# A hybrid four-mixer trunk on one core: segment decays by ScalarE's rectifier, state-space chunks two slots later, a weight panel split earlier, decay sums moved, and the first input transposed by quarters

## The reference, cut to what matters

```python
cs = jnp.cumsum(dt * a, axis=2)
seg = cs_t[..., :, None] - cs_t[..., None, :]
decay = jnp.exp(jnp.where(causal, seg, -jnp.inf))
y_intra = jnp.einsum('bcgjls,bcsgjp->bclgjp', cb[:, :, :, None] * decay, xdt)
```

## Time and profile before

| | us |
|---|---|
| median of 3 runs (lowest to highest) | 1979.54 (1978.78 to 1980.86) |
| the profiled execution | 1979.62 |
| its span, first to last instruction | 1977.6 |
| TensorE (PE) busy | 1930.4 (98% of the span) |
| VectorE (DVE) busy | 1164.7 (59%) |
| ScalarE (ACT) busy | 965.1 (49%) |
| GpSimd (POOL) busy | 491.9 (25%) |
| mean granted TensorE clock | 0.995 of full |

### The profile page before, as it was taken

The page is one execution under the profiler, slowest core; times in us unless marked ns, Lnnn a source line. Parts: engine busy times, 40 slices in busy tenths (PEclk is TensorE's granted clock), DMA queues, the critical chain, the costliest instruction groups (busy, mean ns, idle before and its releaser), DMA issues.

```text
span 1977.6 us, 27606 instructions
## 1 busy us (share of the span) xinstructions
PE 1930.4 (98%) x11112; PEld 1055.3 (53%) x11112; DVE 1164.7 (59%) x1475; ACT 965.1 (49%) x1796; POOL 491.9 (25%) x298
## 2 busy tenths in 40 slices
PE   7999999999999999999999999999999999999998
PEld 3446665455456665544454466654554556655443
DVE  5677676477435765534366777663873366764432
ACT  5674433356325666533356743433653356665331
POOL 0213445043212231121002143541331222221110
PEclk9999999999999999999999999999999999999999
DMA  6224232333334443243211242323433343432431
GB/s 190 81 96 127 98 117 76 117 98 106 107 101 123 123 118 91 87 148 131 68 65 65 96 139 90 113 94 103 118 102 106 101 135 91 123 107 86 140 106 43
DMA packets 204520, 208.92 MB, mean 106 GB/s; under 512 B 28688, under 2 KB 193514, under 8 KB 204394
## 3 DMA queue, kind: packets, MB, share of 16 engines
q1 hardware_dynamic: 204394, 207.17, 33.3%
HBM read 181.91 MB, written 2.16 MB: 93 GB/s over the span
## 4 chain that ended last, share of the span: by engine, by line
PE 84%; DVE 8%; ACT 4%; issue 3%; DMA 1%; SPq 0%; POOL 0%; DVEq 0%; ACTq 0%
PE PS L553 82%; DVE wsp L1259 2%; DVE M L1259 2%; DVE X L1262 1%; PE PS L741 1%; PE PS L659 1%; ACT X L965 1%; DVE ys L1259 1%; PE PS L791 1%; DVE Y L1262 0%; DVE ys L1437 0%; ACT wsp L962 0%; ACT M L995 0%; DMA xres<-x 0%; ACT Y L965 0%
## 5 line engine op out<-in xcount | busy, mean ns | idle before, releaser
L553 PE MATMUL PS<-hT,wsp 128*128 128x512 f16 (+2 forms) x4968 | 1086.1, 377 | 5.1 <-DVE wsp L1259 5.1
L553 PEld LDWEIGHTS PS<-hT,wsp 128*128 128x128 f16 x4968 | 479.9, 98 | 563.1 <-issue 14.0
L1259 DVE SCALAR_TENSOR_TENSOR wsp<-stage,wsp 128x2048 f16<-128x2048 f32 x148 | 377.0, 2547 | 197.8 <-ACT wsp L962 195.1
L553 PE MATMUL PS<-ys,wsp 128*128 128x512 f16 x1536 | 340.4, 379 | 0.0
L962 ACT ACTIVATE wsp<-stage 128x2048 f16<-128x2048 f32 x148 | 281.6, 1903 | 84.2 <-PE PS L553 81.9
L553 PEld LDWEIGHTS PS<-ys,wsp 128*128 128x128 f16 x1536 | 149.6, 98 | 176.4 <-issue 3.0
L553 PE MATMUL PS<-wsp,hT 128*128 128x256 f16 x1728 | 195.5, 273 | 0.0
L553 PEld LDWEIGHTS PS<-wsp,hT 128*128 128x128 f16 x1728 | 168.9, 98 | 22.9 <-issue 2.3
L1601 POOL TENSOR_TENSOR X<-X,K 128x1024 f32<-128x1024 f32 x26 | 63.4, 2440 | 366.7 <-DMA X<-X 366.7
L1601 POOL TENSOR_TENSOR M<-M,T 128x512 f32<-128x512 f32 x48 | 67.4, 1409 | 348.7 <-DVE T L1259 348.7
L965 ACT ACTIVATE X<-PS 128x512 f32<-128x512 f32 x120 | 68.9, 595 | 133.6 <-PE PS L553 99.9
(11 more groups left out here) (197 smaller groups left out, 2107.8 us busy)
## 6 DMA issues: line engine op xcount, KB each, us to landing
stage<-w_in SPq DMA_DIRECT2D x120, 1024.0 KB, 4.9
stage<-w_branch SPq DMA_DIRECT2D x32, 1024.0 KB, 5.1
X<-X SPq DMA_DIRECT2D x120, 128.0 KB, 2.3
stage<-w_out SPq DMA_DIRECT2D x8, 1024.0 KB, 5.3
Y<-sums SPq DMA_DIRECT2D x8, 512.0 KB, 5.8
M<-sums SPq DMA_DIRECT2D x8, 512.0 KB, 5.8
Y<-Y SPq DMA_DIRECT2D x24, 128.0 KB, 2.4
xres<-x SPq DMA_DIRECT2D x4, 512.0 KB, 6.7
```

The costliest lines, as they stand in the source:

```text
L553: return pe.matmul(o, a, b, start=start, stop=stop, skip_group_check=True)
L1259: return dve.scalar_tensor_tensor(out=o, in0=a, scalar=c, in1=b, op0=op0, op1=op1)
```

## The change

- The rows of sums go to ScalarE: eight rectifiers a chunk (`falls`) make max(0, cs of the partition - cs of the column), in place, with a scale of -1 and cs as per-partition bias; the exponential then has the scale -1. Where the mask is one this is the same value; elsewhere it is exp(0) = 1, which the masked C.B product multiplies by zero. POOL's `segments` is gone. `falls` of the next chunk stands at the end of ScalarE's slot.
- Chunks move to slots 18 to 21 and 23 to 26, the ends of the groups to 22 and 27.
- The decay sums move from slot 3 to slot 9, with SyncE's write and reads of the rows, and the waits on their readers from the gates of slot 4 to the transposes of slot 10.
- Panel 2 is split in slot 0, after both evacuations; the softplus chain comes after it on VectorE, and on ScalarE too.
- The input: the first quarter of x is loaded ahead of the constants, ScalarE copies the column parameters after the first square, TensorE transposes six blocks quarter by quarter.
- In `DIFF_END` slots the dummy exponential comes right after the square root, and `rotated_hi` after the squares.

The list of semaphores and the counts per layer, which follow from this, are left out.

```diff
@@ -91,8 +91,8 @@
 ROTATED = ("kc", "qc", "qd", "kd")
-SSD_SLOT = [16, 17, 18, 19, 21, 22, 23, 24]
-SSD_END = {20: 0, 25: 1}
+SSD_SLOT = [18, 19, 20, 21, 23, 24, 25, 26]
+SSD_END = {22: 0, 27: 1}
 TURN_OF = {SLOT[("conv", _i)] + (2 if _i == 8 else 1): _i for _i in (8, 0, 2, 4, 6)}
@@ -106,9 +106,9 @@
 
-SUMS_IN = SLOT[("ga", 1)]
+SUMS_IN = SLOT[("conv", 10)]
 ROWS_OUT_AT = SUMS_IN + 5
-ROWS_IN_AT = {SLOT[("vc", 0)] + 1: 0, SLOT[("vc", 0)] + 3: 1}
+ROWS_IN_AT = {SUMS_IN + 6: 0, SUMS_IN + 7: 1}
 ROWS_IN_AT.update({SSD_SLOT[_q] + 3: _q + 2 for _q in range(6)})
@@ -153,7 +153,9 @@
 
-    if p == 0 or p + 1 >= OUT0:
+    if p == 0:
+        return range(LOAD_OF[2], LOAD_OF[3])
+    if p == 1 or p + 1 >= OUT0:
         return range(0)
@@ -460,10 +462,11 @@
         def _(sp):
-            sp.dma_start(K[:, 0:K_COS], consts[:, 0:K_COS]).then_inc(s["consts_in"], 16)
-            load_columns(sp, 0)
             for q in range(ST):
                 sp.dma_start(xres[:, q, :], x[0, q * P:q * P + P, :]).then_inc(x_in[q], 16)
+                if q == 0:
+                    sp.dma_start(K[:, 0:K_COS], consts[:, 0:K_COS]).then_inc(s["consts_in"], 16)
+                    load_columns(sp, 0)
             sp.dma_start(stage[:, 0], panel_source(0, 0)).then_inc(s["first_in"], 16)
@@ -713,8 +716,8 @@
                     if p == SUMS_IN:
-                        pe.wait_ge(s["lru_v"], at("lru_v", 2, layer))
-                        pe.wait_ge(s["lru_w"], at("lru_w", 2, layer))
+                        pe.wait_ge(s["lru_v"], at("lru_v", 8, layer))
+                        pe.wait_ge(s["lru_w"], at("lru_w", 8, layer))
                         pe.wait_ge(s["dta_ready"], at("dta_ready", 1, layer))
@@ -764,9 +767,6 @@
                                 pe.wait_ge(s["dta_ready"], at("dta_ready", 1, layer))
-                            if t == 2:
-                                pe.wait_ge(s["dec_ready"], at("dec_ready", 1, layer))
-                                pe.wait_ge(s["cs_rows"], at("cs_rows", 1, layer))
                             if t >= 2:
@@ -781,7 +781,8 @@
                             if n == 0:
-                                pe.wait_ge(s["lru_w"], at("lru_w", 8, layer))
+                                pe.wait_ge(s["dec_ready"], at("dec_ready", 1, layer))
+                                pe.wait_ge(s["cs_rows"], at("cs_rows", 1, layer))
                             if n >= 2:
@@ -840,21 +841,27 @@
 
-                    if k == 0:
-                        pe.wait_ge(s["xn_ready"], at("xn_ready", 4, 0))
-                        pe.wait_ge(s["first_cols"], at("first_cols", 2, 0))
-                    if k >= 6:
-                        pe.wait_ge(s["whole_lo"], k - 5)
+                    pe.wait_ge(s["whole_lo"], k - 5)
                     for q in range(ST):
...
 
+                def turn_quarter(q):
+
+                    pe.wait_ge(s["xn_ready"], at("xn_ready", q + 1, 0))
+                    if q == 0:
+                        pe.wait_ge(s["first_cols"], at("first_cols", 2, 0))
+                    for k in range(6):
+                        one = pe.transpose(whole_at(k)[:, P * q:P * q + P], Mseq[:, q, k * P:k * P + P], ident)
+                        if q == ST - 1:
+                            one.then_inc(s["whole_T"], 1)
+
                 def first_product():
...
                         return wsp[:, 0, h, k, P * u:P * u + P]
-                    for k in range(6):
-                        turn_whole(k)
+                    for q in range(ST):
+                        turn_quarter(q)
                     pe.wait_ge(s["first_hi"], at("first_hi", 1, 0))
@@ -932,8 +939,8 @@
             square_x(0)
+            start_columns(act, 0)
             square_x(1)
-            start_columns(act, 0)
             square_x(2)
@@ -1017,10 +1024,10 @@
                         q = SSD_SLOT.index(p)
-                        act.wait_ge(s["ssd_tri"], at("ssd_tri", q + 1, layer))
                         if q > 0:
                             act.wait_ge(s["ssd_out"], at("ssd_out", q, layer))
-                        act.activation(est, seg[q % 2], ACT.Exp).then_inc(s["ssd_exp"], 1)
+                        act.wait_ge(s["ssd_fall"], at("ssd_fall", q + 1, layer))
+                        act.activation(est, seg[q % 2], ACT.Exp, scale=-1.0).then_inc(s["ssd_exp"], 1)
                     if p in SSD_END:
@@ -1085,6 +1092,7 @@
                         act.activation(mean, mean, ACT.Sqrt, scale=1.0 / P, bias=eps).then_inc(s["df_sq"], 1)
+                        act.activation(small[:, 100:101], eps, ACT.Exp)
 
@@ -1142,10 +1150,10 @@
                             copy(Y_HI[1][:, f, :], PS[:, 4 + t, :], colB[:, B_NG + f:B_NG + f + 1]).then_inc(s["yb_hi"], 1)
-                    if p > 0 and PANELS[p - 1][0] in ROTATED:
+                    turned = p > 0 and PANELS[p - 1][0] in ROTATED
+                    if turned and p not in DIFF_END:
                         rotated_hi(p)
                     if p in DIFF_END:
-                        act.activation(small[:, 100:101], eps, ACT.Exp)
                         act.wait_ge(s["df_nT"], at("df_nT", 2 * DIFF_END[p] + 2, layer))
@@ -1156,6 +1164,8 @@
                                 .then_inc(s["df_or"], 1)
+                    if turned and p in DIFF_END:
+                        rotated_hi(p)
 
@@ -1170,7 +1180,22 @@
 
+                def falls(q):
+
+                    g, c = divmod(q, 4)
+                    act.wait_ge(seg_in[q % 2], at("seg_in0", 16 * (q // 2 + 1), layer))
+                    if q == 0:
+                        act.wait_ge(s["cs_ready"], at("cs_ready", 1, layer))
+                    for j in range(8):
+                        last = act.activation(seg[q % 2][:, j, :], seg[q % 2][:, j, :], ACT.Relu, scale=-1.0,
+                                              bias=cs[:, c, 8 * g + j:8 * g + j + 1])
+                    last.then_inc(s["ssd_fall"], 1)
+
                 def after(p):
+                    if p + 1 == SSD_SLOT[0]:
+                        falls(0)
+                    if p in SSD_SLOT[:-1]:
+                        falls(SSD_SLOT.index(p) + 1)
                     if SWA0 < p <= SWA0 + 8:
@@ -1191,15 +1216,21 @@
                     local_turned(p)
-                    for n in splits_in(p):
-                        split_hi(n)
+                    if p > 0:
+                        for n in splits_in(p):
+                            split_hi(n)
                     before(p)
                     evacuate(p, 0)
+                    if p == 0:
+                        evacuate(p, 1)
+                        for n in splits_in(p):
+                            split_hi(n)
                     between(p)
...
                         turned_hi(act, nxt, 0)
-                    evacuate(p, 1)
+                    if p > 0:
+                        evacuate(p, 1)
                     after(p)
@@ -1549,9 +1580,14 @@
                     evacuate(p, 0)
+                    if p == 0:
+                        evacuate(p, 1)
+                        for n in splits_in(p):
+                            split_lo(n)
                     between(p)
                     middle(p)
-                    evacuate(p, 1)
+                    if p > 0:
+                        evacuate(p, 1)
                     after(p)
@@ -1607,17 +1643,6 @@
 
-                def segments(q):
-
-                    g, c = divmod(q, 4)
-                    here = cs[:, c, 8 * g:8 * g + 8].unsqueeze(2).to_broadcast([P, 8, P])
-                    if q == 0:
-                        pool.wait_ge(s["cs_ready"], at("cs_ready", 1, layer))
-                    pool.wait_ge(seg_in[q % 2], at("seg_in0", 16 * (q // 2 + 1), layer))
-                    tt(seg[q % 2], seg[q % 2], here, ALU.subtract).then_inc(s["ssd_diff"], 1)
-                    pool.wait_ge(s["ssd_diff"], at("ssd_diff", q + 1, layer))
-                    tt(seg[q % 2], seg[q % 2], tri.unsqueeze(1).to_broadcast([P, 8, P]), ALU.mult).then_inc(s["ssd_tri"], 1)
-
                 def rotated_lo(p):
@@ -1662,10 +1687,6 @@
                         tt(xw, xdt, head(dend[:, c, hs]), ALU.mult).then_inc(s["ssd_x"], 1)
-                        if q < 7:
-                            segments(q + 1)
-                    if p + 1 == SSD_SLOT[0]:
-                        segments(0)
                     if p > 0 and PANELS[p - 1][0] in ROTATED:
```

More of the change, by code:

```diff
@@ L125 @@
     "rope_stack": 576, "rows_in": 16, "second_in": 16, "sp_exp": 1, "sp_in": 1, "ssd_T": 8, "ssd_exp": 8, "ssd_g": 8,
-    "ssd_mt": 8, "ssd_norm": 2, "ssd_out": 8, "ssd_read": 8, "ssd_ss": 2, "ssd_st": 6, "ssd_tri": 8, "ssd_diff": 8, "ssd_x": 8,
+    "ssd_mt": 8, "ssd_norm": 2, "ssd_out": 8, "ssd_read": 8, "ssd_ss": 2, "ssd_st": 6, "ssd_fall": 8, "ssd_x": 8,
     "ssd_y": 8, "step_in": 16, "sw_T": 16, "sw_Ta": 16, "sw_e": 16, "sw_m": 16, "sw_n": 16, "sw_o": 16, "sw_s": 16,
@@ L341, in program @@
```

(6 more changed lines are left out.)

## The result

The changed kernel takes 1946.2 us (median of 4 runs, 1944.91 to 1947.35) against 1979.16 us for the kernel before, run beside it (4 runs): ratio 0.9833, 95% interval 0.9816 to 0.985. The forecast was 1950. The profiled execution took 1947.35 us, its span is 1945.4 us, and the span is 32.2 us shorter than before.

A forecast was written before the change was run, and what follows sets the result against it. TensorE was taken as the bound, with 47.2 us idle and low-clock matmuls to win. Terms 0.9 + 0.6 + 3.0 + 7.6 + 10.6 + 7.0 = 29.7 us off 1979.6 gave 1950, range 1945 to 1963.

The forecast's parts named there:

- What bounds it: TensorE, busy 1930.4 of 1977.6 us; the change can win only from 47.2 us idle time and low-clock matmuls.
- Start: Input loads and transposes by quarters: three quarters transposed while x arrives, first products end earlier; gain 0.9 us.
- Panel 2: Split in slot 0: gain 0.6 us in layer 0, 3.0 in layer 1 after a new 2.0 us step-size wait.
- Decay sums: Moved to slot 9: removes the 2.00 us waits and slow gates of slot 4 in both layers; gain 7.6 us.
- Chunks: State-space stages: later slots and segments off POOL remove TensorE's waits there in both layers; gain 10.6 us.
- I count all 10.6 us: State-space waits, all counted as gone: 5.0 + 2.0 before transposes, 2.2 before normalized outputs, 1.4 for low halves.
- Rectifiers: Eight a chunk on ScalarE: 2.5 us, within 4.3 us of room before TensorE takes up the chunk's result.
- The slower rival: ScalarE bounds the chunks: TensorE waits at ten late chunks' exponentials above 0.54 us a rectifier, 1987 at 1.0 us; chance 0.03.
- Head pairs: Slots 53 and 57, both layers: earlier table load and later rotary copies remove four 1.74 us waits; gain 7.0 us.
- VectorE and the place had made the chunks late: Rival for the chunks: VectorE, not POOL's segments, made them late; gives back 5 to 10 us, 1955 to 1961; chance 0.20.
- a wait takes the place of each one removed: Rival, at slot 4's gates and head-pair ends: new waits replace the old, about 1963 to 1975; chance 0.10.

The follow-up runs named there:

- Run 7: Changed kernel with panel 2 split in slot 1 again instead of slot 0: 1949.02 us.
- run 2: Changed kernel with the chunks back in slots 16 to 19 and 21 to 24, rectifiers kept on ScalarE: 1954.22 us.
- run 3: Changed kernel with the segments back on POOL in the new slots, no rectifiers on ScalarE: 1952.45 us.
- run 8: Changed kernel with each rectifier in two halves of 64 columns, sixteen a chunk: 1953.64 us.
- the better version: Changed kernel with chunk 4's rectifiers at the end of slot 22 and slot 2's gates asked for four k-steps later: 1940.16 us (median of 5 runs).
- run 6: Changed kernel with the decay sums back in slot 3, row loads left in their new slots: 1952.6 us.
- run 12: Changed kernel unchanged, executed again beside the better version: 1946.63 us (4 runs).

## Why the prediction was right, and where it wasn't

**What bounds it**: right. The gain is idle time of TensorE (24.3 us) and shorter busy time (7.9 us), most of it low clock.

**Start**: I took 0.9 us of gain, with -1.0 to +1.0 as bounds. It is 1.1 with the products at full clock and 0 with them at the low one; the loss of 1.0 did not come. The step that three quarters of the transposes are done while x still arrives was wrong: one quarter is (six at 7.00 us), since the second quarter's square could start at 9.50 us only and the last three come together.

**Panel 2**: the chain of steps held, with the split ahead, the softplus late and a new wait of 2.0 us (2.2 measured). The size was off by the clock: I forecast net 3.0 with 5.0 as the bound for a clock that stays up; it stayed up in the first execution, 4.7, and fell in the second, 4.7 - 1.8 = 2.9. Run 7 gives 3.1 for the split's place alone; the rest of the 4.7 is the early evacuation of tile 1, which I had not priced by itself, and how long the low clock lasted.

**Decay sums**: 8.0 for 7.6, and nothing late behind their new place in slot 9. Undone, 7.7, of which 6.2 at the gates of slot 4.

**Chunks**: the step "I count all 10.6 us" failed in one term and was short in another. The term that failed is L799's 2.2 us: I let the wait for the normalized outputs go with POOL's segments, and did not ask what the rectifiers of the next chunk stand in front of at the end of group 0. It is there now with 1.73 us a layer, 3.9 us in time. I had read `evacuate` as passing at once where VectorE takes the tile; it does not. That this stage still gained 11.6, close to the 10.6, is luck: two things that I had not priced made up for it. A wait costs 0.2 to 0.4 us more than its length, and in the kernel before, the 1.98 us wait in layer 1 slot 17 had low clock behind it (the 15 us window there reads 0.89), which I had looked for at slot 4 only:

```profile
1221.03 1.06 PE L791 MATMUL PS<-K,M 128*128 128x128 f32 x8 [1.98 <-DVE Y L1262]
1221.93 2.67 PE L553 MATMUL PS<-hT,wsp 128*128 128x512 f16 x6
```

Six such products took 1.47 us at full clock, in slot 2 of layer 0. The reason given, POOL beside VectorE, is the smaller half of the stage's gain (runs 2 and 3); the larger is the place.

**Rectifiers**: 2.43 us a chunk for 2.5; no reload of a table; room of 4.1 us for 4.3, as run 8 shows. The slower rival (over 0.54 us each) had its place wrong as well: with sixteen instructions the queue becomes too long at the end of group 0, not at a chunk's exponential. By the rule of the Trainium skill (ScalarE: Activation LUTs, Rules for kernel authors) a rectifier belongs on VectorE; no run here has it there. What the runs show is that 2.43 us a chunk on ScalarE in place of 5.6 us on POOL is worth 3.9 us in the chunk stages of both layers.

**Head pairs**: 8.0 for 7.0. The small waits of 0.3 us, which I had left standing, mostly went too, and each 1.74 us wait cost 1.9.

**The other rivals.** That VectorE and the place had made the chunks late is true of the larger half: had the chunks stayed in their slots, 5.2 us of the gain would have gone, the lower end of what this rival gives back. That a wait takes the place of each one removed was true for two of them, L800 and the step sizes, 5.7 us of waiting, and the better version takes both away.

What stays open: why the clock falls behind some waits of 2 us and not behind others, how long it then stays low, and whether work on TensorE at the start would keep its clock up.

## What to carry to other kernels

Where a queue is in order, ask of every operation you add what stands behind it, at its worst place and not at the mean one: eight 0.30 us rectifiers left no wait behind them in seven places of a layer and cost 1.9 us in the eighth. A wait at the top of a helper holds its engine even where the engine has nothing to do there; an idle time that the profile puts down to "issue" with no releaser is where to look for one. When the bounding engine has a wait, first ask whether the same engine could do other work there: four k-steps of the slot's own products ahead of the gates cost nothing and gave 2.4 to 4.2 us.

## What the runs showed of the hardware

- **The clock behind a wait of 2 us is a matter of the execution.** Waits of TensorE of 1.98 to 2.31 us were followed by low clock in 8 of 19 cases: both at slot 4 and one of two at slot 17 in the kernel before, one of two at slot 4 in run 6, one of two at the end of group 0 in run 2, and three of eleven in layer 1 slot 2 of the changed kernel and its variants (runs 2, 3 and 12), where the same program paid once and once not. No wait of 1.0 to 1.83 us was followed by it, and all four of 3.2 to 4.5 us were (run 8 twice, run 7, and layer 1 slot 2 in the kernel before). Where it falls behind a wait of 2 us, it adds 1.7 to 1.8 us. A removed wait of 2 us is thus worth 2.3 or 4.0 us. The spread of times fits, though the runs are few: the five runs of the better version lie within 1.3 us, the four of the changed one within 2.6.
- **The granted-clock column reads 1.00 at the start** where products take 631 ns and not 379. There it is the durations that tell the level. By the Trainium skill (TensorE: Matmul & The Clock Gate, What's actually happening) the array starts at its low clock and the same kernel shows different numbers of slow matmuls from run to run; the trace agrees, with 4 executions of 12 slow at the same place.
- **An activation's cost is mostly its start**: 0.39 us for 128 columns, 0.335 for 64, and 0.30 for each of eight of 128 columns behind each other.
